# Evacuating, splitting and turning in the projection phases of an encoder layer: block copies, reordered query units, and half swaps done by transfers

## The reference

```
h = rms_norm(x, norm_mix_pre[l]);  z = h @ w_in[l]
a_q, a_kv, a_kr, b_q, b_k, b_v, c_q, c_k, c_v = split(z)      # widths 256,128,32, 3 x 256, 512,128,128

# group A, latent attention, 4 heads
q  = rms_norm(a_q, q_lora_norm) @ w_uq        # (256) -> 4 x (64 plain + 32 rotary)
kv = rms_norm(a_kv, kv_norm) @ w_ukv          # (128) -> 4 x (64 key + 64 value)
q_rot, k_rot = apply_rope(q[..., 64:], ang), apply_rope(a_kr, ang)

# group C, 8 query heads, 2 key heads of width 64
q = axial_rope(rms_norm(c_q, c_q_norm));  k = axial_rope(rms_norm(c_k, c_k_norm))

apply_rope(x): x1, x2 = halves of x;  concat([x1*cos - x2*sin, x2*cos + x1*sin])
```

## Time and profile before

| | us |
|---|---|
| median of 3 runs (3768.0 to 3770.8) | 3770.79 |
| the profiled execution | 3768.39 |
| its span in the trace | 3766.6 |
| PE busy in the span | 3660.8 (97%) |
| DVE busy | 1843.0 (49%) |
| ACT busy | 1568.9 (42%) |
| POOL busy | 1141.5 (30%) |

### The profile page before, as it was taken

The page is one execution under the profiler, slowest core; times in us unless marked ns, Lnnn a source line. Parts: engine busy times, 40 slices in busy tenths (PEclk is TensorE's granted clock), DMA queues, the critical chain, the costliest instruction groups (busy, mean ns, idle before and its releaser), DMA issues. The chain is left out here.

```text
span 3766.6 us, 49891 instructions
## 1 busy us (share of the span) xinstructions
PE 3660.8 (97%) x18327; PEld 3020.0 (80%) x18327; DVE 1843.0 (49%) x2914; ACT 1568.9 (42%) x2531; POOL 1141.5 (30%) x827
## 2 busy tenths in 40 slices
PE   8999999989999999999989999999899999999998
PEld 7777777768788888888767877777787888888886
DVE  4133878954543333434541357689464333434335
ACT  4334877974312212221342357789642222221213
POOL 1233453433412122121342244434343122121123
PEclk9999999999999999999999999999999999999999
DMA  5412221113111111111323222211231111111113
GB/s 165 126 56 81 72 64 25 39 40 119 55 34 35 44 39 39 33 41 37 112 66 121 70 77 76 55 32 33 68 101 36 43 39 39 33 41 37 33 45 112
DMA packets 203404, 227.43 MB, mean 60 GB/s; under 512 B 14688, under 2 KB 163206, under 8 KB 203207
## 3 DMA queue, kind: packets, MB, share of 16 engines
q1 hardware_dynamic: 203247, 225.37, 20.0%
HBM read 173.86 MB, written 51.48 MB: 60 GB/s over the span
## 5 line engine op out<-in xcount | busy, mean ns | idle before, releaser
L220 PE MATMUL ps<-hh,wh 128*128 128x512 f32 (+1 forms) x2688 | 970.0, 361 | 26.7 <-PEq L214 17.1
L221 PE MATMUL ps<-hl,wh 128*128 128x512 f32 (+1 forms) x2688 | 955.8, 356 | 0.0
L222 PE MATMUL ps<-hh,wl 128*128 128x512 f32 (+1 forms) x2688 | 954.8, 355 | 0.0
L2447 POOL TENSOR_TENSOR wl<-raw,wh 128x1024 fp32r<-128x1024 f32 x126 | 301.7, 2401 | 1267.2 <-ACT wh L2280 1267.2
L220 PEld LDWEIGHTS ps<-hh,wh 128*128 128x128 f32 x2688 | 510.9, 190 | 105.4 <-issue 23.5
L221 PEld LDWEIGHTS ps<-hl,wh 128*128 128x128 f32 x2688 | 511.0, 190 | 76.8 <-issue 5.7
L2508 DVE SCALAR_TENSOR_TENSOR cb<-ps,params,cb 128x1023 f32<-128x1023 f32 (+1 forms) x172 | 143.9, 878 | 870.4 <-ACT cb L2289 870.4
L222 PEld LDWEIGHTS ps<-hh,wl 128*128 128x128 f32 x2688 | 510.0, 190 | 72.5
L1538 DVE TENSOR_TENSOR pl<-ps,ph 128x512 fp32r<-128x512 f32 (+1 forms) x576 | 375.2, 652 | 55.0 <-ACT ps L1383 54.6
L1492 DVE TENSOR_REDUCE mx<-ps 128x1 f32<-128x512 f32 x480 | 330.6, 689 | 141.7 <-PE ps L1297 82.8
L1382 ACT ACTIVATE ph<-ps 128x512 fp32r<-128x512 f32 (+1 forms) x576 | 329.7, 572 | 158.4 <-PE ps L1263 153.3
(11 more groups left out here) (254 smaller groups left out, 5684.2 us busy)
## 6 DMA issues: line engine op xcount, KB each, us to landing
raw<-in_w_up SPq DMA_DIRECT2D x88, 512.0 KB, 3.9
heads<-stage SPq DMA_DIRECT2D x38, 640.0 KB, 3.5
raw<-in_w_down SPq DMA_DIRECT2D x44, 512.0 KB, 3.7
rq<-heads SPq DMA_DIRECT2D x56, 320.0 KB, 4.8
raw<-in_w_in SPq DMA_DIRECT2D x32, 512.0 KB, 5.0
rk<-heads SPq DMA_DIRECT2D x32, 320.0 KB, 4.7
raw<-in_w_out SPq DMA_DIRECT2D x16, 512.0 KB, 4.3
residual<-my SPq DMA_DIRECT2D x32, 256.0 KB, 2.1
```

The source lines that it names most:

```text
L220: pe.matmul(out, wh, xh, start=(k == 0), stop=False)
L221: pe.matmul(out, wh, xl, start=False, stop=False)
L222: last = pe.matmul(out, wl, xh, start=False, stop=(k == len(pairs) - 1))
L2447: pool.tensor_tensor(c.wl[slot][:], c.raw[parity][:], c.wh[slot][:].bitcast(F32), ALU.subtract).then_inc(w_lo, units)
```

## The change

In the latent phase:

- Unit 0 is copied out of PSUM by DVE in three blocks (`first_copied`), unit 1 by ACT; the squares are then taken by ACT from the SBUF copies. PE's unit 2 waits for the copy block by block. ACT no longer loads its function table in this phase.
- The key/value weights get tiles of their own (`kv_raw`, `kv_hi`, `kv_lo`), so slot 1 is free for head unit 1 from the start, and slot 0 once the query units are done. The splits of head units 1 and 0 follow ACT's copies of output units 1 and 3.
- The first query unit goes ahead of the turn of the rotary key; on DVE the low part of the key latent goes ahead of the rotary key's arithmetic.

In the head phase:

- The permutation matmul goes. SP swaps the halves with eight transfers of 16 partitions x 1280 from `stage` to `rot` for each of the five units, and DVE multiplies `rot` by the sine table in one instruction. The sign sits in the table now (`sin_c`).
- The norm sums alternate between banks 6 and 7, and wait for the squares alone.

```diff
-                pe.wait_ge(evacuated, 1)
-                project(pe, c, 0, 0).then_inc(w_used, 1)
+                for b, (t0, w) in enumerate(BLOCKS):
+                    pe.wait_ge(first_copied, b + 1)
+                    last = product(pe, bank(c, b, w), [... for k in range(KC)])
+                last.then_inc(w_used, 1)
...
-                pe.wait_ge(evacuated, 4)
-                for b, (t0, w) in enumerate(BLOCKS):
-                    aux(6 + b, [(c.perm_a[0:32, 0:32], c.stage[0][0:32, t0:t0 + w])], slice(0, 32), w)
                 for j, (unit, col, chunks, row) in enumerate(outs):
                     m = 4 + j
-                    pe.wait_ge(w_lo, unit - 3)
+                    pe.wait_ge(q_lo if unit == 4 else kv_lo, 1)
                     pe.wait_ge(lat_lo, 1 + max(chunks))
-                    pe.wait_ge(evacuated, m - 1)
+                    pe.wait_ge(evacuated, m - 2)
...
                     if j == 0:
-                        continue
+                        pe.wait_ge(evacuated, 3)
+                        for b, (t0, w) in enumerate(BLOCKS):
+                            aux(6 + b, [(c.perm_a[0:32, 0:32], c.stage[0][0:32, t0:t0 + w])], slice(0, 32), w)
...
-                act.preload_act_table_set(LOG_SET)
...
+                act.activation(c.lat[1][:], unit_psum(c, 1), ACT.Copy).then_inc(evacuated, 1)
+                act.wait_ge(first_copied, 3)
+                act.activation(c.psq[0][:], c.lat[0][:], ACT.Square).then_inc(squared, 1)
+                act.wait_ge(evacuated, 1)
+                act.activation(c.psq[1][:], c.lat[1][:], ACT.Square).then_inc(squared, 1)
+                act.wait_ge(kv_arrived, 32)
+                act.activation(c.kv_hi[:], c.kv_raw[:], ACT.Copy).then_inc(kv_hi, 1)
+                for b in range(3):
+                    sums(b, b, 256)
...
-                    if j in (3, 7):
+                    if j in (1, 3):
+                        i = (1, None, 0)[j - 1]
+                        act.wait_ge(head_arrived[i], 16)
+                        act.activation(c.wh[i][:], c.raw[i][:], ACT.Copy).then_inc(head_hi, 1)
...
+                for t0, w in BLOCKS:
+                    dve.tensor_copy(c.lat[0][:, t0:t0 + w], unit_psum(c, 0, t0, t0 + w)).then_inc(first_copied, 1)
...
+                def turn(n):
+                    r = n - ROPED[0]
+                    sp.wait_ge(evacuated, n + 1)
+                    if r >= 2:
+                        sp.wait_ge(roped, r - 1)
+                    for g in range(0, P, 16):
+                        from_row = g + 16 if g % 32 == 0 else g - 16
+                        sp.dma_start(c.rot[n % 2][g:g + 16, :], c.stage[n % 3][from_row:from_row + 16, :]).then_inc(turned[n % 2], 16)
+
                 for n in range(2, UNITS):
+                    if n - 4 in ROPED:
+                        turn(n - 4)
                     load_weights(sp, c, n, c.raw[n % 2][:], head_unit(c, L, n), raw_arrived, w_lo, 2)
                     if n >= 4:
                         store(n - 4)
...
-                    pe.matmul(bank(c, 6, w), c.block_ones[:], c.psq[n % 2][:, t0:t0 + w], start=True, stop=True).then_inc(unit_sum, 1)
-                    if 3 * r + b >= 1:
-                        pe.wait_ge(turn_read, 3 * r + b)
-                    pe.matmul(bank(c, 7, w), c.perm_c[:], c.stage[n % 3][:, t0:t0 + w], start=True, stop=True).then_inc(turned, 1)
+                    pe.matmul(bank(c, 6 + (r + b) % 2, w), c.block_ones[:], c.psq[n % 2][:, t0:t0 + w], start=True, stop=True).then_inc(unit_sum, 1)
...
-                    for b, (t0, w) in enumerate(BLOCKS):
-                        dve.wait_ge(turned, 3 * r + b + 1)
-                        dve.tensor_tensor(rot[:, t0:t0 + w], bank(c, 7, w), c.sin[:, t0:t0 + w], ALU.mult).then_inc(turn_read, 1)
+                    dve.wait_ge(turned[n % 2], 128 * (r // 2 + 1))
+                    dve.tensor_tensor(rot[:], rot[:], c.sin[:], ALU.mult).then_inc(turn_read, 1)
```

More of the change, by code:

```diff
@@ L145, in place_buffers @@
     c.latl = take("latl", [P, 3, T], F32R)
+    c.kv_raw = take("kv_raw", [P, 512])
+    c.kv_hi, c.kv_lo = take("kv_hi", [P, 512], F32R), take("kv_lo", [P, 512], F32R)
     assert at[0] <= end
@@ L673, in _ @@
                     src = c.w_uq[bass.ds(L, 1), k * P:k * P + P, :].rearrange("a p (h n) -> (a p) h n", h=H_A)
-                    dst = wide[4](c.raw[0]).rearrange("p (k n) -> p k n", k=2)[:, k, :]
-                    sp.dma_start(dst[:, 0:P].rearrange("p (h n) -> p h n", h=H_A), src[:, :, 64:96]).then_inc(raw_arrived[0], 16)
-                    sp.dma_start(dst[:, P:3 * P].rearrange("p (h n) -> p h n", h=H_A), src[:, :, 0:64]).then_inc(raw_arrived[0], 16)
+                    dst = query_part(c.raw[0]).rearrange("p (k n) -> p k n", k=2)[:, k, :]
+                    sp.dma_start(dst[:, 0:P].rearrange("p (h n) -> p h n", h=H_A), src[:, :, 64:96]).then_inc(q_arrived, 16)
+                    sp.dma_start(dst[:, P:3 * P].rearrange("p (h n) -> p h n", h=H_A), src[:, :, 0:64]).then_inc(q_arrived, 16)
                 src = c.w_ukv[bass.ds(L, 1), :, :].rearrange("a p (h n) -> (a p) h n", h=H_A)
                 for part in range(2):
[L679 to L684, removed]
+                    dst = c.kv_raw[:, 256 * part:256 * part + 256].rearrange("p (h n) -> p h n", h=H_A)
+                    sp.dma_start(dst, src[:, :, 64 * part:64 * part + 64]).then_inc(kv_arrived, 16)
+                sp.dma_start(c.raw[1][:], head_unit(c, L, 1)).then_inc(head_arrived[1], 16)
+                sp.wait_ge(q_lo, 1)
+                sp.dma_start(c.raw[0][:], head_unit(c, L, 0)).then_inc(head_arrived[0], 16)
                 sp.wait_ge(roped, 1)
@@ L690, in _ @@
                 for j in range(2, 8):
-                    sp.wait_ge(evacuated, 4 + j)
+                    sp.wait_ge(evacuated, 3 + j)
                     row = outs[j - 1][3]
@@ L707, in aux @@
                     last.then_inc(aux_done, 1)
-                pe.wait_ge(evacuated, 1)
-                project(pe, c, 0, 0).then_inc(w_used, 1)
+                for b, (t0, w) in enumerate(BLOCKS):
+                    pe.wait_ge(first_copied, b + 1)
+                    last = product(pe, bank(c, b, w),
+                                   [(c.wh[0][:, k, :], c.wl[0][:, k, :], c.hh[:, k, t0:t0 + w], c.hl[:, k, t0:t0 + w]) for k in range(KC)])
+                last.then_inc(w_used, 1)
                 pe.wait_ge(squared, 2)
@@ L756, in sums @@
                     act.activation(c.pr[:, t0:t0 + w], c.pln[:, t0:t0 + w], ACT.Exp, scale=-0.5).then_inc(root, 1)
[L758 to L768, removed]
+                act.activation(c.lat[1][:], unit_psum(c, 1), ACT.Copy).then_inc(evacuated, 1)
[7 more added lines that the diff above has]
+                    sums(b, b, 256)
+                act.wait_ge(w_used, 1)
+                act.activation(c.psq[0][:], unit_psum(c, 0), ACT.Square).then_inc(squared, 1)
+                act.activation(c.lat[2][:], unit_psum(c, 0), ACT.Copy).then_inc(evacuated, 1)
+                act.wait_ge(q_arrived, 64)
+                act.activation(query_part(c.wh[0]), query_part(c.raw[0]), ACT.Copy).then_inc(q_hi, 1)
                 for i in range(2):
@@ L958, in _ @@
                     if n - 1 in ROPED:
-                        project(pe, c, n % 2, n % 2, lambda b: norm_and_turn(n - 1, b)).then_inc(w_used, 1)
-                        norm_and_turn(n - 1, 2)
+                        project(pe, c, n % 2, n % 2, lambda b: norm(n - 1, b)).then_inc(w_used, 1)
+                        norm(n - 1, 2)
                     else:
@@ L974, in roots @@
                             act.wait_ge(roped, r)
-                        act.activation(c.pln[:, t0:t0 + w], bank(c, 6, w), ACT.Ln, scale=1.0 / 64, bias=c.eps[:]).then_inc(sum_read, 1)
+                        act.activation(c.pln[:, t0:t0 + w], bank(c, 6 + (r + b) % 2, w), ACT.Ln, scale=1.0 / 64, bias=c.eps[:]).then_inc(sum_read, 1)
                         act.wait_ge(sum_read, x + 1)
@@ L1087, in _ @@
                     first_values(part)
-        end_phase(nc, raw_arrived + [w_hi, w_lo, w_used, tables, evacuated, squared, unit_sum, turned, sum_read, turn_read,
-                                     root, cos_done, added, roped, head0] + stored)
+        end_phase(nc, raw_arrived + [w_hi, w_lo, w_used, tables, evacuated, squared, unit_sum, sum_read, turn_read,
+                                     root, cos_done, added, roped, head0] + stored + turned)
 def attention(nc, c, L):
```

60 lines of the change are left out of this document (30 added, 30 removed).

## The result

The changed kernel takes 3733.55 us (median of 4, 3729.73 to 3736.56) against 3770.8: a ratio of 0.9902, 95% interval 0.9885 to 0.992. The forecast was 3727 in a range of 3715 to 3743: faster as said, 37 us instead of 44. The profiled execution, the slowest of the four, took 3736.56, 31.8 less than that of before.

What follows compares the result with a forecast made beforehand. PE was taken as busy nearly the whole span. Latent phases 18.8, clock 2.1 and head phase 21.8 sum to 42.7 us off 3768.4, giving 3725.7; half of 2.4 added makes 3727, range 3715 to 3743.

Steps and rivals of the forecast that it cites:

- The head phase: Ten head units with norm and turn each lose one fp32 set of 2.18 us on PE: 21.8 us.
- The chain of the swaps: Head phase: swapped rows in `rot` 14.7 us after a unit's end, slack 2.6 us, so swaps stay hidden.
- The start: Start of the latent phase: PE begins at about 71.75 in place of 74.71, gaining 3.0 us.
- The tail: End of the latent phase: barrier 3.0 us sooner, 0.4 from one split fewer between short units; sum 3.4.
- The middle: Latent phase around the rotary key's turn: second query unit ends at 121.4 in place of 124.39, gaining 3.0 us.
- If the middle stall still brings one, I lose 1.7 a layer: Clock loss if PE's wait before the turn's third block still brings a slow stretch; half of it was counted.
- +2.1 us of clock: Slow-clock stretches behind PE's waits: half of 7.4 us possible gain less 1.6 for the middle; bounds -3.4 and +7.4.
- latents give half: Rival, chance 0.15: hidden pacing in the latent tail or ACT at key/value weights; loss some 5 us a layer, 3737.
- My sign for it: A phase border only 6 us sooner, not 11, would mean ACT's pace in the latent tail was missed.
- Late swaps: Rival, chance 0.07: head-phase swap chain of 22.2 us a unit against 16; 32 us lost in all, 3759.
- swaps that stop the phase: Rival, chance 0.03: head-phase swap issues at 3.30 us, chain 39 us a unit; slower, at 3895.
- One reading ahead of the forecast: Barrier ahead of L220, 17.1 us in four places, taken as roughly both borders of each layer's latent phase.

Runs made afterwards that it cites:

- Late splits: The changed kernel with the splits of head units 1 and 0 behind ACT's copies of output units 3 and 7, not 1 and 3: 3743.51 us.
- the runs where I forecast 20.9: The changed kernel's latent phase with the head phase and sine table of the kernel before: 3754.17 us, ratio 0.9958.

## Why the prediction was right, and where it missed

The head phase: 2.18 us a set was forecast, 18.14 - 15.97 = 2.17 measured; 21.8 us forecast, 21.8 by the two head phases of the run that had that change alone and 19.3 by its median. What the alternating banks of the sums are worth by themselves was not tried. The chain of the swaps held too, though both its pieces were off: an issue takes 0.67 us, not 0.4 (eight in 5.34), and the rows are there 2.0 us after the last issue, not 4. The sum, 7.3 us, is what I had, and the slack 2.3 us against 2.6.

The start: 3.0 us forecast, 4.58 - 1.65 = 2.9 measured, and the clock came back in layer 0 as I had thought possible (1.00 over 71 to 78).

The tail: 3.4 forecast. From the second query unit's copy to the next phase it is 15.70 us, before 143.10 - 124.59 = 18.51: 2.8. Late splits cost just that.

The middle is the step that failed, in two terms. From the rotary key's copy to the second query unit's it takes 15.49 us where it took 14.40: a loss of 1.1 in place of a gain of 3.0, 4.1 us in layer 0 (3.6 in layer 1).

The first term is a duration. I said "so PE stands from 115.7 to 117.5: 1.8 us"; PE stood 3.43 us, and the third block began 9.1 us behind the rotary key's copy in place of 7.3, in both layers. I had kept 1.85 us for DVE's scaling, from a place where DVE started ahead of POOL's product and shared only the last 0.5 us of its weight split. The change brought POOL's product forward by the weight split that used to precede it, so it starts 0.7 us ahead of DVE, and the scaling takes 3.57. Moving POOL alone brought back 1.55. I had weighed that exclusion for the swaps and not here, one phase earlier, where the same two engines meet. Behind it stands the new DVE order, the low part ahead of the turn's multiplies; undoing that alone took the wait to 0.62. I had counted that order in, at 1.5 us, but not asked what it bought: nothing waited for the low part.

The second term is the clock behind that wait. The forecast had 4.1 us from the third block's start to the second query unit's copy, all at 2.4 GHz. It took 6.4 us in layer 0 (granted clock 0.54 over 115 to 120) and 5.9 in layer 1. I had named this loss, "If the middle stall still brings one, I lose 1.7 a layer", and counted half of it. It came in both layers, at 2.3 and 1.8 us, and the run with POOL's product later puts it at 3.0 with a wait below my 1.8. So the 3.0 us of gain needed a clock that my own stall would likely have taken away.

With it the forecast's +2.1 us of clock, which counted the border behind the phase too, was wrong in its sign for the latent phases. The two starts gave 2.1 us beyond their waits (to the rotary key's copy 4.5 and 3.4 us less, of which 2.9 each were the wait), the two middles took 4.1. Term by term for both layers, forecast against the profiled executions: start 6.0, 5.8; middle without the clock 6.0, 2.4; tail 6.8, 5.6; clock +2.1, -2.0; in all 20.9, 11.8. These are the terms of the slowest of the four executions, which gained 32 us; the median gained 37, and only the profiled one can be split like this. What decides whether a short wait brings the fall stays open.

Of the rivals, "latents give half" is nearest in size, 11.9 us by the profiled phases and 15 by the runs where I forecast 20.9, but for another reason than its own: stages whose stores are late paced the tail only once the middle had been mended. My sign for it misled as well. The border came 6 us sooner, which I had set down to ACT's pace in the tail; the tail gave 2.8 of its 3.4 us, and it was the middle. Late swaps, and swaps that stop the phase, did not happen.

One reading ahead of the forecast was wrong without harm: of the 17.1 us of barrier in the earlier trace rows only 11.2 are borders of a latent phase (5.5 and 5.7, at its end); the other two places, 5.9 us, lie elsewhere in the layers and are the same in the changed kernel.

## What to carry to other kernels

A duration holds only for the order in which it was measured: when a change brings a POOL instruction forward, look at what DVE starts just behind it, and add the overlap. A wait of PE that is left in the stream costs its own length and the slow clock that may follow; here the second part was as large as the first, so a forecast with such a wait needs both. When work is moved ahead of a wait to fill it, check what the instruction waited for now stands behind, on its own engine. A matmul that only permutes rows can be had from transfers, here at eight issues of 0.67 us on a queue that was mostly idle, if the result isn't wanted within some 8 us.

## What the runs showed of the hardware

A DVE instruction with several SBUF tiles of 128x1280 that starts behind a POOL one isn't slowed down but held: POOL ends at 107.35 + 2.92 = 110.27, and 1.36 us later DVE is done, where it takes 1.55 alone. That remainder does not depend on how long the two overlap. It is 1.35 us in the kernel before (POOL's weight split ends at 113.27, DVE at 114.62, 0.5 us of overlap) and 1.35 us with the swaps issued twice (POOL's product ends at 221.76, DVE's 4.12 us add at 223.11, 2.8 us of overlap). The profile counts the time held as the instruction's own and names no wait for POOL. In the kernel before, DVE was at work when POOL's product began, and POOL took 4.14 us for what takes 2.92 now. So the order decides who pays. The Trainium skill, "SBUF — State Buffer", section "SBUF: two separate sides", says that of a DVE instruction with two SBUF inputs and a POOL one that reads SBUF, the one that starts second is blocked until the first is done; these rows agree.

TensorE's clock fell behind short waits too, but not behind each: behind the turn's small fp32 matmuls and a wait of 0.62 us in both layers, behind 1.41 us in layer 0 and not in layer 1 of one kernel, and not behind 1.65 us at the start of layer 0. With no wait at all in the middle it held in both layers.

An SBUF to SBUF transfer of 16 partitions by 5120 bytes cost SP a median of 0.59 us to issue (0.51 to 0.97), more than a store of 128 partitions (0.34), and landed in 2.6 us (2.5 to 3.5).
